# First branch's projection inside the last four attention rounds; value products one round back in three attentions

## Chip, cores and metric

The kernel runs on one core of one Trainium2 chip. The metric is the device time of one execution in microseconds. The kernel before was timed three times: median 3740.02 us, lowest 3732.03, highest 3750.38. The profile is of a fourth execution.

## What is computed

Batch 1, 256 tokens, width 1024. Four layers, fp32, in two blocks. The first block's two layers are feed-forward, mixer, feed-forward; the second block's two are mixer, mixture of experts. Only the mixers are touched by the change. Cut to what matters:

```python
# first block, layer 0 ("ab") and layer 1 ("cd"): 8 heads of 64
o = softmax(q k^T ...) @ v
x = x + m * (concatenate([att, conv]) @ w_out)

# second block, both layers
def mixer(h, ...):
    qa, ka, va, ub, qc, kc, vc, gates = split(h @ w_in)      # 28 slabs of 256 columns
    a = softmax(qk of map 0) - lam * softmax(qk of map 1)     # 4 heads, causal
    y_a = rms_norm(a @ va, subln_g) * (1 - lambda_init) @ w_proj_a
    y_b = silu(layer_norm(conv(glu(ub)))) @ w_proj_b + b_proj_b
    y_c = stick_breaking(qc, kc, vc) @ w_proj_c               # 8 heads
    g = sigmoid(gates)
    merged = g[0] * y_a + g[1] * y_b + g[2] * y_c
    return merged @ w_out
```

All layers also need modulation vectors: 9 (6 in the second block) vectors of 1024 per layer, each the product of a condition vector with a matrix from HBM.

## The kernel before

The program has ten sections s = 0 to 9, one after the other: ffn, ab, ffn, ffn, cd, ffn, mix2, moe, mix2, moe. Here "short mixers" are sections 1 (ab) and 4 (cd), written by `mixer1`; "long mixers" are sections 6 and 8, written by `mixer2`. Each engine has its own program, written by hand in the order in which the engine runs it, with semaphores between them (`wait_ge`, `then_inc`). What stands earlier in an engine's program always runs earlier. The activations lie transposed: 128 features on the partitions, 256 tokens along the row.

**Weights.** SyncE loads slabs of 1 MB into a ring of six slots, in program order; a slot is loaded again when the projection that read it six slabs before has signalled `proj_done`. In a long mixer slabs 0 to 27 are `w_in`, 28 and 29 the two halves of `w_proj_a`, 30 and 31 `w_proj_b`, 32 and 33 `w_proj_c`, 34 to 37 `w_out`. Results go to the PSUM banks 4 to 7 in turn: unit j to bank 4 + j % 4. Before unit j, TensorE waits for `proj_taken` (unit j - 4 has been read out of that bank). A long mixer's units 28 to 31 are the first branch (y_a), 32 to 35 the second, 36 to 39 the third; a unit is 8 matmuls.

**Short mixers' attention** (L1054 to L1090, ScalarE L1682 to L1691, VectorE L2269 on). For each of 8 heads: score of the next head, half a slab of `w_in` (rounds 0 to 5), four transposes of this head's probabilities (`turn_probs`, L1037) into bank 2, a copy of bank 2 to `pT` by ScalarE (`copy_turned`, L1660), and two value products from `pT` into bank 3 (`value`, L1075). In round 7 of section 1 the column sums of the next section's modulation (L891, 48 trace records) stand before the transposes.

**Long mixers' first attention** (L1153 to L1179). The same for four heads: scores of the next two maps, one whole slab (20 + i), transposes, value products (L1174), then slab 24, and the sums of squares of the output (`pairs`, L1029), which ScalarE squares first (L1641).

**Long mixers' second attention** (L1192 to L1212; VectorE `soft` L2466 on, L2485, L2490; ScalarE L1745 to L1771). Eight rounds i. TensorE: three suffix sums (L1200 to L1202), scores of head i + 2 (L1187, for i < 6), half a slab (L1205, for i < 4), and then a wait for `fin`, the product of VectorE (L2490) from which the value products (L1211) are made. VectorE, in rounds 0 to 3, ends with `scale_heads` (L2463, L2464), which finishes the first branch's input `ya` and signals `suba`; in rounds 4 to 7 with one modulation step (`add_mods`, L1992).

**Three projections** (L1214 to L1233). After the eight rounds TensorE runs the 12 units (L1231). VectorE (L2496 to L2519) first waits for `gsig`, ScalarE's sigmoid over the gates of branches 1 and 2 (L1774), and then takes unit after unit. In branch 0 each of its eight products (L2506) is followed by a modulation step, where there is one left: section 6 has eight left, section 8 none. In section 8 the column sums of the next modulation are split over two places of this stretch.

**Modulation steps.** GpSimd loads rows of `w_mod` (512 KB) into two buffers `wmod`, in turn (L821); a buffer is loaded again when VectorE has done the step that read it (`mod_step`).

Of the kernel before, what the change touches and what calls it, by code (L numbers as in the profile page):

```python
# [28 lines left out]
ACT = mybir.ActivationFunctionType  # L29
# [3 lines left out]
P = 128  # L33
# [207 lines left out]
def build(nc, A, out):  # L241
    ctx = ExitStack()
    with ctx:
# [582 lines left out]
        def _(pe):  # L826
# [213 lines left out]
            def mixer1(sec, X):  # L1040
# [40 lines left out]
                for i in range(NQ):  # L1081
# [8 lines left out]
                    value(i)  # L1090
# [31 lines left out]
            def mixer2(sec, X):  # L1122
# [36 lines left out]

                probs = lambda i: pb[:, (2 * i) % 4]  # L1160
# [3 lines left out]
                for i in range(4):  # L1164
# [5 lines left out]
                    pe.wait_ge(*X("pT_done", i + 1))  # L1170
                    if i:
                        pe.wait_ge(*X("o_taken", i))
                    for b in range(TB):
                        ins = pe.matmul(bank[3][:, 0:T], va(b, i), pT[:, i % 2, b, :], start=(b == 0), stop=(b == TB - 1))  # L1174
                    ins.then_inc(X["pv_done"], 1)
                slab(24)
# [3 lines left out]
                def z_scores(i):  # L1180
# [7 lines left out]
                    ins.then_inc(X["zs"], 1)  # L1188

# [4 lines left out]
                for i in range(8):  # L1194
# [10 lines left out]
                    if i < 4:  # L1205
                        slab(26 + i // 2, (i % 2,))
                    pe.wait_ge(*X("fin", i + 1))
# [6 lines left out]
                for br_, (ready, count, src) in enumerate((("suba", 4, ya), ("lnd", 1 + CT, glu), ("o_taken", 8, yc))):  # L1214
                    pe.wait_ge(*X(ready, count))
                    for half in range(2):
                        q = slabs[28 + 2 * br_ + half]
                        here(q)
                        w = proj_slab(q[0])
                        if (br_, half) == (1, 1) and s == 8:  # L1220
                            pe.wait_ge(*X("o_taken", 8))
                            pe.wait_ge(mod_step, MOD_STEPS * 9)
                            sum_columns(9, range(0, MODT // 2), 3)
                        if (br_, half) == (2, 0) and s == 8:
                            sum_columns(9, range(MODT // 2, MODT), 3, MODT // 2).then_inc(mod_summed, 1)
                        for m in range(4):
                            j = 28 + 4 * br_ + 2 * half + m // 2
                            if m % 2 == 0:
                                pe.wait_ge(proj_taken, taken0 + j - 3)
                            for k in range(CT):  # L1230
                                ins = pe.matmul(bank[4 + j % 4][:, (m % 2) * T:(m % 2 + 1) * T], w[:, k, m * P:(m + 1) * P], src[:, k, :], start=(k == 0), stop=(k == CT - 1))  # L1231
                            if m % 2:
                                ins.then_inc(proj_done, 1)  # L1233
# [1547 lines left out]
```

## Time and profile before

| | |
|---|---|
| median of 3 runs | 3740.02 us (3732.03 to 3750.38) |
| the profiled execution's own time | 3743.29 us |
| its span in the trace | 3741.5 us |
| mean granted TensorE clock | 0.969 of full speed |
| TensorE matmul busy | 3523.4 us (94%) |
| VectorE busy | 2328.0 us (62%) |
| ScalarE busy | 1464.8 us (39%) |
| moved by DMA | 842.64 MB, mean 225 GB/s |

The busy time of a pipelined engine counts a matmul from its issue to its modelled end, so rows of one group overlap: sixteen fp32 records of 128x256 take 3.62 us in a row of the timeline, but the next row starts 3.45 us after it. What a stretch costs is read from start to start. One fp32 matmul instruction of the program shows as two records, a transpose as one. In the timeline a bracket at a row's end gives the idle time before it and who ended it.

### The profile page before, as it was taken

To read this page: it belongs to the slowest core of one execution; us is meant where nothing else is said; L and a number is where in the kernel's file an instruction comes from. 1 tells how busy PE (TensorE), PEld (TensorE's weight loads), DVE (VectorE), ACT (ScalarE), POOL (GpSimd) and SP (SyncE) were. 2 spreads that over 40 slices of the span, in tenths; PEclk is the share of its full clock that TensorE was granted. 3 is DMA by queue.
4 is the path that set the end of the run, shared out by engine and by line. 5 is a ranking of instruction groups with operands and counts; after the bars stand their busy time and mean duration, and the time that the engine had idled before them with its cause. 6 is when DMAs were issued, how large, how long until landed. Compare 5 with 4: busy or idle time off the path is not lost.

```text
span 3741.5 us, 52688 instructions
## 1 busy us (share of the span) xinstructions
PE 3523.4 (94%) x21065; PEld 2988.2 (80%) x21065; DVE 2328.0 (62%) x3525; ACT 1464.8 (39%) x2213; POOL 246.2 (7%) x337
## 2 busy tenths in 40 slices
PE   4999999999899999899999999999888999999999
PEld 2998899997699877789777776778778977767776
DVE  6774476775477574456666666647454766666666
ACT  1432333432243214133555555531232345555554
POOL 3010010010001100000000000000000000000000
PEclk9999899999899999889999999999998999999999
DMA  7785385784278652345999989875322688999986
GB/s 265 254 293 184 98 285 191 253 299 151 76 259 297 208 169 93 133 157 181 295 302 299 297 266 297 282 241 169 132 84 92 214 272 277 295 282 299 296 278 197
DMA packets 580321, 842.64 MB, mean 225 GB/s; under 512 B 22715, under 2 KB 489760, under 8 KB 578832
## 3 DMA queue, kind: packets, MB, share of 16 engines
q1 hardware_dynamic: 514508, 665.85, 54.4%
q0 software_dynamic: 41056, 147.35, 11.7%
q10 hardware_dynamic: 24548, 26.57, 2.6%
q8 instruction: 141, 2.31, 0.3%
q14 instruction: 68, 0.56, 0.0%
HBM read 836.37 MB, written 3.33 MB: 224 GB/s over the span
## 4 chain that ended last, share of the span: by engine, by line
PE 75%; DVE 11%; DMA 8%; ACT 4%; issue 2%; SPq 1%; DVEq 0%; ACTq 0%
PE bank L1007 12%; PE bank L912 11%; PE bank L914 11%; PE bank L913 11%; PE bank L1366 8%; DMA ring<-in_w 3%; DMA far_up<-in_w 3%; DVE work L2400 2%; PE bank L1335 2%; PE bank L1379 2%; PE bank L1336 2%; PE bank L1231 2%; PE bank L1330 2%; PE bank L891 1%; PE bank L1331 1%
## 5 line engine op out<-in xcount | busy, mean ns | idle before, releaser
L914 PE MATMUL bank<-hh,ring_lo 128*128 128x256 f32 (+1 forms) x2176 | 621.2, 285 | 0.0
L912 PE MATMUL bank<-hh,hi 128*128 128x256 f32 (+1 forms) x1984 | 571.4, 288 | 13.2 <-issue 10.2
L913 PE MATMUL bank<-h_lo,hi 128*128 128x256 f32 (+1 forms) x1984 | 566.3, 285 | 0.0
L1007 PE MATMUL bank<-h,ring 128*128 128x256 f32 x2432 | 554.2, 388 | 7.4 <-DVE h L2513 3.9
L1007 PEld LDWEIGHTS bank<-h,ring 128*128 128x128 f32 x2432 | 474.0, 195 | 79.1 <-issue 7.0
L914 PEld LDWEIGHTS bank<-hh,ring_lo 128*128 128x128 f32 (+1 forms) x2176 | 419.3, 193 | 0.0
L912 PEld LDWEIGHTS bank<-hh,hi 128*128 128x128 f32 (+1 forms) x1984 | 382.2, 193 | 27.6 <-issue 21.3
L913 PEld LDWEIGHTS bank<-h_lo,hi 128*128 128x128 f32 (+1 forms) x1984 | 382.3, 193 | 1.4 <-issue 1.4
L912 PE MATMUL bank<-hid,hi 128*128 128x256 f32 (+1 forms) x1216 | 347.2, 286 | 1.1 <-DVE ring_lo L2660 1.1
L913 PE MATMUL bank<-hid_lo,hi 128*128 128x256 f32 (+1 forms) x1216 | 344.6, 283 | 0.0
L914 PE MATMUL bank<-hid,ring_lo 128*128 128x256 f32 (+1 forms) x1088 | 308.4, 283 | 0.0
L2655 DVE TENSOR_TENSOR ring_lo<-ring,hi_far 128x1024 fp32r<-128x1024 f32 x176 | 209.1, 1222 | 64.2 <-ACT hi_far L1817 63.6
L2126 DVE TENSOR_TENSOR ring_lo<-ring,hi 128x1024 fp32r<-128x1024 f32 (+1 forms) x180 | 209.3, 1199 | 55.0 <-ACT hi L1559 54.9
L912 PEld LDWEIGHTS bank<-hid,hi 128*128 128x128 f32 (+1 forms) x1216 | 233.9, 192 | 1.4 <-issue 1.2
L913 PEld LDWEIGHTS bank<-hid_lo,hi 128*128 128x128 f32 (+1 forms) x1216 | 233.9, 192 | 0.0
L2655 DVE TENSOR_TENSOR ring_lo<-ring,hi 128x1024 fp32r<-128x1024 f32 x168 | 199.8, 1222 | 41.9 <-ACT hi L1817 40.9
L1992 DVE SCALAR_TENSOR_TENSOR macc<-wmod,cond,macc 128x1024 f32<-128x1024 f32 x126 | 160.8, 1282 | 102.4 <-DMA wmod<-in_w_mod 88.5
L821 POOL DMA_DIRECT2D wmod<-in_w_mod x216 | 114.2, 529 | 1663.5 <-DVE macc L1992 963.3
L1559 ACT ACTIVATE hi<-ring 128x1024 fp32r<-128x1024 f32 (+1 forms) x180 | 180.5, 1035 | 110.2 <-DMA ring<-in_ffn_w 84.4
L795 POOL DMA_INDIRECT got<-rows_scratch,slot_tok x98 | 98.5, 1005 | 1700.4 <-PE bank L1317 1258.2
L914 PEld LDWEIGHTS bank<-hid,ring_lo 128*128 128x128 f32 (+1 forms) x1088 | 209.3, 192 | 0.0
L1817 ACT ACTIVATE hi_far<-ring 128x1024 fp32r<-128x1024 f32 x176 | 178.2, 1057 | 66.1 <-DMA ring<-in_w 66.1
(382 smaller groups left out, 6700.1 us busy)
## 6 DMA issues: line engine op xcount, KB each, us to landing
ring<-in_w SPq DMA_DIRECT2D x258, 1024.0 KB, 9.1
ring<-in_ffn_w SPq DMA_DIRECT2D x120, 1024.0 KB, 6.7
wmod<-in_w_mod POOLq DMA_DIRECT2D x216, 512.0 KB, 5.5
far_up<-in_w SPq DMA_DIRECT2D x84, 1024.0 KB, 11.3
ring<-in_w_in SPq DMA_DIRECT2D x74, 1024.0 KB, 5.2
work<-in_w SPq DMA_DIRECT2D x42, 1024.0 KB, 7.2
ring<-in_w_out SPq DMA_DIRECT2D x16, 1024.0 KB, 5.1
ring<-in_w_mod SPq DMA_DIRECT2D x12, 1024.0 KB, 12.1
```

What stands on the lines that cost most here:

```text
L795: pool.indirect_dma_start(got[0:m, p % 2, :], None, rows_dram[l].ap(), bass.IndirectOffsetOnAxis(slot_tok[0:m, rank - WIDE_FROM:rank - WID ...
L821: pool.dma_start(wmod[:, q % 2, :], w[l][k][:, at:at + D]).then_inc(mod_full[q % 2], 16)
L912: pe.matmul(o, w_hi, x_hi, start=start, stop=False, skip_group_check=True)
L913: pe.matmul(o, w_hi, x_lo, start=False, stop=False, skip_group_check=True)
L914: return pe.matmul(o, w_lo, x_hi, start=False, stop=stop, skip_group_check=True)
L1007: ins = pe.matmul(o[:, half * T:(half + 1) * T], l_, r_, start=(k == 0), stop=(k == KD - 1))
L1366: ins = pe.matmul(bank[2 + half][0:m, :], hidden_few[p % 2][:, c * m:(c + 1) * m], w[:, c, half * 512:(half + 1) * 512], start=(c == 0), s ...
L1559: act.activation(up_hi(j, t, m), up_half(slots[j], t, m), ACT.Copy).then_inc(hi_done, 1)
L1817: act.activation(up_hi(j, t, P, n % 2), unit_up(slot)[:, j, :, t * P:(t + 1) * P], ACT.Copy).then_inc(hi_done, 1)
L1992: dve.scalar_tensor_tensor(out=acc, in0=w, scalar=c, in1=acc, op0=ALU.mult, op1=ALU.add).then_inc(mod_step, 1)
L2126: dve.tensor_tensor(up_half(slots[j], t, m, ring_lo), up_half(slots[j], t, m), up_hi(j, t, m), ALU.subtract).then_inc(lo_done, 1)
L2655: dve.tensor_tensor(unit_up(slot, True)[:, j, :, c], unit_up(slot)[:, j, :, c], up_hi(j, t, P, n % 2), ALU.subtract).then_inc(lo_done, 1)
```

## The change

Three edits.

1. Short mixers: `value(i - 1)` comes behind `turn_probs(i)`, and `value(7)` behind the loop; ScalarE takes the results one round later (`take_values`).
2. Long mixers' first attention: the same, with `value(3)` between the two halves of slab 24.
3. Long mixers' second attention: in rounds 4 to 7 units 28, 29, 30 and 31 of the first branch's projection stand before the wait for `fin`, where rounds 0 to 3 have half a slab. The rest of the projections follows the loop as before. VectorE waits for `gsig` before branch 1 and no longer before branch 0.

```diff
@@ mixer1, TensorE
                     turn_probs(X, i, probs(i))
-                    value(i)
+                    if i:
+                        value(i - 1)
+                value(NQ - 1)
...
@@ mixer2, TensorE
+                def value(i):
+                    pe.wait_ge(*X("pT_done", i + 1))
+                    if i:
+                        pe.wait_ge(*X("o_taken", i))
+                    for b in range(TB):
+                        ins = pe.matmul(bank[3][:, 0:T], va(b, i), pT[:, i % 2, b, :], start=(b == 0), stop=(b == TB - 1))
+                    ins.then_inc(X["pv_done"], 1)
...
                     slab(20 + i)
                     turn_probs(X, i, probs(i))
-                    pe.wait_ge(*X("pT_done", i + 1))
                     if i:
-                        pe.wait_ge(*X("o_taken", i))
-                    for b in range(TB):
-                        ins = pe.matmul(bank[3][:, 0:T], va(b, i), pT[:, i % 2, b, :], start=(b == 0), stop=(b == TB - 1))
-                    ins.then_inc(X["pv_done"], 1)
-                slab(24)
+                        value(i - 1)
+                slab(24, (0,))
+                value(3)
+                slab(24, (1,))
...
+                def project(br_, half, src, pairs_of):
+
+                    q = slabs[28 + 2 * br_ + half]
+                    here(q)
+                    w = proj_slab(q[0])
+                    for pair in pairs_of:
+                        j = 28 + 4 * br_ + 2 * half + pair
+                        pe.wait_ge(proj_taken, taken0 + j - 3)
+                        for m in (2 * pair, 2 * pair + 1):
+                            for k in range(CT):
+                                ins = pe.matmul(bank[4 + j % 4][:, (m % 2) * T:(m % 2 + 1) * T], w[:, k, m * P:(m + 1) * P], src[:, k, :], start=(k == 0), stop=(k == CT - 1))
+                        ins.then_inc(proj_done, 1)
...
                     if i < 4:
                         slab(26 + i // 2, (i % 2,))
+                    else:
+
+                        pe.wait_ge(*X("suba", 4))
+                        project(0, (i - 4) // 2, ya, (i % 2,))
                     pe.wait_ge(*X("fin", i + 1))
...
-                for br_, (ready, count, src) in enumerate((("suba", 4, ya), ("lnd", 1 + CT, glu), ("o_taken", 8, yc))):
...
+                pe.wait_ge(*X("lnd", 1 + CT))
+                project(1, 0, glu, (0, 1))
+                if s == 8:
+                    pe.wait_ge(*X("o_taken", 8))
+                    pe.wait_ge(mod_step, MOD_STEPS * 9)
+                    sum_columns(9, range(0, MODT // 2), 3)
+                project(1, 1, glu, (0, 1))
+                pe.wait_ge(*X("o_taken", 8))
+                if s == 8:
+                    sum_columns(9, range(MODT // 2, MODT), 3, MODT // 2).then_inc(mod_summed, 1)
+                for half in range(2):
+                    project(2, half, yc, (0, 1))
                 pe.wait_ge(*X("merged", 1))
@@ mixer1, ScalarE
+                def take_values(n):
+
+                    act.wait_ge(*X("pv_done", 2 * n + 2))
+                    act.activation(att[:, n, :], bank[3][:, 0:T], ACT.Copy).then_inc(X["o_taken"], 1)
...
                     copy_turned(X, i, i - 1 if i >= 2 else 0)
+                    if i in (2, 4, 6):
+                        take_values(i // 2 - 1)
                     if i in (1, 3, 5):
                         take(sec, 6 + i // 2)
-                    if i % 2:
-                        act.wait_ge(*X("pv_done", i + 1))
-                        act.activation(att[:, i // 2, :], bank[3][:, 0:T], ACT.Copy).then_inc(X["o_taken"], 1)
+                take_values(NQ // 2 - 1)
@@ mixer2, ScalarE
                     copy_turned(X, i, i - 1 if i >= 2 else 0)
-                    act.wait_ge(*X("pv_done", i + 1))
-                    act.activation(ya[:, i, :], bank[3][:, 0:T], ACT.Copy).then_inc(X["o_taken"], 1)
+                    if i:
+                        take_values(i - 1)
+                take_values(3)
@@ mixer2, VectorE
-                dve.wait_ge(*X("gsig", 1))
                 for br_ in range(3):
+                    if br_ == 1:
+                        dve.wait_ge(*X("gsig", 1))
```

The order of instructions at the places of which the prediction speaks. In section 1, TensorE, the end of the last attention round and the start of the output projection (L891 are the column sums, L1037 the transposes, L1075 the value products, L1007 the output projection), a piece of the difference:

```order
 L891 MATMUL bank<-mats,macc 128x1 x24
 L1037 MATMUL bank<-mats,pb 128x128 x4
-L1075 MATMUL bank<-pT,vp 128x256 x2
+L1075 MATMUL bank<-pT,vp 128x256 x4
 L1007 MATMUL bank<-work,ring 128x256 x4
 L1007 MATMUL bank<-h,ring 128x256 x4
```

The value products of heads 6 and 7 now stand together behind the last transposes.

In section 6, TensorE, from the value products of round 5 of the second attention to the projections, before (L1200 to L1202 suffix sums, L1211 value products, L1231 projections, L1007 the output projection):

```order
L1211 MATMUL bank<-pT,vp 128x256 x2
L1200 MATMUL bank<-work,mats 128x256
L1201 MATMUL bank<-work,mats 128x256
L1202 MATMUL bank<-work,mats 128x256
L1211 MATMUL bank<-pT,vp 128x256 x2
L1200 MATMUL bank<-work,mats 128x256
L1201 MATMUL bank<-work,mats 128x256
L1202 MATMUL bank<-work,mats 128x256
L1211 MATMUL bank<-pT,vp 128x256 x2
L1231 MATMUL bank<-work,ring 128x256 x96
L1007 MATMUL bank<-h,ring 128x256 x48
```

The same place with the change (L1221 to L1223 are the suffix sums, L1236 the value products, L1208 the projections):

```order
L1236 MATMUL bank<-pT,vp 128x256 x2
L1221 MATMUL bank<-work,mats 128x256
L1222 MATMUL bank<-work,mats 128x256
L1223 MATMUL bank<-work,mats 128x256
L1208 MATMUL bank<-work,ring 128x256 x8
L1236 MATMUL bank<-pT,vp 128x256 x2
L1221 MATMUL bank<-work,mats 128x256
L1222 MATMUL bank<-work,mats 128x256
L1223 MATMUL bank<-work,mats 128x256
L1208 MATMUL bank<-work,ring 128x256 x8
L1236 MATMUL bank<-pT,vp 128x256 x2
L1208 MATMUL bank<-work,ring 128x256 x64
```

Eight of the projection's matmuls stand ahead of each value product of rounds 6 and 7, as in rounds 4 and 5 ahead of this piece, and 64 are left behind the rounds where there were 96.

## Rows read from the trace of the kernel before

**Rows 1.** Page: the chain that ended last, share of the span by engine.

```profile
PE 75%; DVE 11%; DMA 8%; ACT 4%; issue 2%; SPq 1%; DVEq 0%; ACTq 0%
```

**Rows 2.** Source view of L1075: idle before it (both TensorE rows), us, times.

```profile
  ACT pT L1660: 26.1, 32
```

**Rows 3.** TensorE timeline, section 1, round 0: start, duration, operation, records, [idle].

```profile
345.46 3.62 PE L1007 MATMUL bank<-h,ring 128*128 128x256 f32 x16
348.91 0.60 PE L1037 MATMUL bank<-mats,pb 128*128 128x128 f32 x4
350.20 1.13 PE L1075 MATMUL bank<-pT,vp 128*128 128x256 f32 x4 [0.69 <-ACT pT L1660]
351.17 0.59 PE L1065 MATMUL bank<-kz,work 128*128 128x256 f32 x2
```

**Rows 4.** TensorE timeline, section 1, rounds 6 and 7, output projection.

```profile
392.19 0.66 PE L1037 MATMUL bank<-mats,pb 128*128 128x128 f32 x4 [1.96 <-DVE pb L2287]
...
395.40 10.24 PE L891 MATMUL bank<-mats,macc 128*128 128x1 f32 x48
405.50 1.09 PE L1037 MATMUL bank<-mats,pb 128*128 128x128 f32 x4
...
409.83 3.78 PE L1007 MATMUL bank<-work,ring 128*128 128x256 f32 x8 [0.47 <-ACT work L1691]
```

**Rows 5.** VectorE timeline, section 4, its wait in a round.

```profile
927.55 0.69 DVE L2273 TENSOR_REDUCE small<-bank 128x2 f32<-128x512 f32 x1 [1.11 <-PE bank L1065]
```

**Rows 6.** TensorE timeline, section 4, the last round's transposes.

```profile
953.64 1.11 PE L1037 MATMUL bank<-mats,pb 128*128 128x128 f32 x4 [2.43 <-DVE pb L2287]
```

**Rows 7.** TensorE timeline, section 6, first attention, round 0.

```profile
1409.74 0.60 PE L1037 MATMUL bank<-mats,pb 128*128 128x128 f32 x4
...
1412.05 1.89 PE L1157 MATMUL bank<-kz,work 128*128 128x256 f32 x8
```

**Rows 8.** ScalarE timeline, section 6: the square behind the last copy.

```profile
1443.34 0.38 ACT L1736 ACTIVATE work<-bank 128x256 f32<-128x256 f32 x1 [1.22 <-PE bank L1174]
1443.76 1.06 ACT L1641 ACTIVATE work<-work 128x1024 f32<-128x1024 f32 x1
```

**Rows 9.** TensorE timeline, section 6, rounds 4 to 7 and projections.

```profile
1488.24 0.59 PE L1200 MATMUL bank<-work,mats 128*128 128x256 f32 x2
...
1493.01 1.13 PE L1211 MATMUL bank<-pT,vp 128*128 128x256 f32 x4 [2.44 <-DVE pT L2490]
...
1506.16 2.07 PE L1211 MATMUL bank<-pT,vp 128*128 128x256 f32 x4 [3.31 <-DVE pT L2490]
...
1513.78 25.48 PE L1231 MATMUL bank<-work,ring 128*128 128x256 f32 x112
...
1547.44 17.10 PE L1231 MATMUL bank<-work,ring 128*128 128x256 f32 x64 [3.37 <-DVE work L2504]
```

**Rows 10.** VectorE timeline, section 6, round 7 and first branch.

```profile
1512.12 1.28 DVE L1992 SCALAR_TENSOR_TENSOR macc<-wmod,cond,macc 128x1024 f32<-128x1024 f32 x1
1519.37 0.42 DVE L2506 TENSOR_TENSOR h<-bank,work 128x256 f32<-128x256 f32 x1 [5.96 <-ACT work L1774]
...
1544.64 1.28 DVE L1992 SCALAR_TENSOR_TENSOR macc<-wmod,cond,macc 128x1024 f32<-128x1024 f32 x1 [4.34 <-issue]
```

**Rows 11.** Windows view, 1506 to 1509: busy per engine (instructions), granted clock, DMA share, GB/s.

```profile
1506.00:1509.00 3.00, 2.84 (x7) 2.28 (x8) 1.30 (x2) 0.00 (x0) 0.53 (x1) 0.50 0.07 12
```

**Rows 12.** Tile view of wmod, 1440 to 1560: time of its loads.

```profile
DMA to landing us min/median/max: 3.5/4.0/6.7
```

**Rows 13.** DMA view, 1513 to 1546: KB each, median us to landing.

```profile
ring<-in_w_out SPq DMA_DIRECT2D x4, 1024.0 KB, 7.1
```

**Rows 14.** TensorE timeline, section 8, round 4, projections, column sums.

```profile
2747.07 0.59 PE L1200 MATMUL bank<-work,mats 128*128 128x256 f32 x2
...
2772.15 22.57 PE L1231 MATMUL bank<-work,ring 128*128 128x256 f32 x96
...
2806.74 14.06 PE L1231 MATMUL bank<-work,ring 128*128 128x256 f32 x64
```

More of the change, by code:

```diff
@@ L1212, in mixer2 @@
                     ins.then_inc(X["pv_done"], 1)
-                for br_, (ready, count, src) in enumerate((("suba", 4, ya), ("lnd", 1 + CT, glu), ("o_taken", 8, yc))):
[L1215 to L1233, printed above, removed]
+                pe.wait_ge(*X("lnd", 1 + CT))
[10 more added lines that the diff above has]
+                    project(2, half, yc, (0, 1))
                 pe.wait_ge(*X("merged", 1))
@@ L1725, in exps, with take_values @@
                     exp_scores(X, pb[:, i % 4], pb[:, i % 4], i % 4, i % 2)
+                def take_values(i):
+                    act.wait_ge(*X("pv_done", i + 1))
+                    act.activation(ya[:, i, :], bank[3][:, 0:T], ACT.Copy).then_inc(X["o_taken"], 1)
                 exps(0)
```

## The prediction

> **What bounds the kernel now.** I read the page's chain first: three quarters of it is TensorE [rows 1], so time is won where TensorE has nothing to do or runs slowly in the mixers. The source view of the short mixers' value products gives 26.1 us of idle time, both TensorE rows counted, in 32 cases: each of the 16 rounds waits for ScalarE's copy of the transposes [rows 2]. The timelines show the size of each place. In a round of section 1 the transposes start at 348.91, the value products at 350.20, the next score at 351.17 [rows 3]. Sixteen records of the slab before them take 3.45 us from start to start where their row says 3.62 [rows 3]; so a record is 0.216 us, a program's matmul 0.43, and the last 0.17 us of a row lie under the next. In rounds 4 to 7 of the second attention there is no slab to run, and TensorE waits 2 to 3 us for VectorE's product (2.44 and 3.31 in the rows) [rows 9]. The windows view shows what else this costs: in one such stretch the granted clock is 0.50, 1.2 of 2.4 GHz [rows 11].
>
> **Short mixers, rounds 0 to 5.** From transposes to next score takes 2.26 us; without the wait it is 0.43 (0.60 less 0.17) and 0.86 (four records), 1.29. That is 0.97 a round, 5.8 us in six rounds. The cover of the copy is the next head's work. In section 1 nothing else is near. In section 4 VectorE idles only 1.11 us a round [rows 5]: the 0.97 just fits.
>
> **Section 1, rounds 6 and 7.** From the transposes of round 6 at 392.19 to the output projection at 409.83: 17.6 us [rows 4], with the 48 records of column sums at half speed (10.24, so 5.1 at full). After: transposes 0.43, value(5) 0.86, column sums between 5.1 and 10.2, I take 7.7, since a 0.7 us gap is gone ahead of them; transposes at half speed 0.86, value(6) and value(7) 1.73 each, 0.7 to ScalarE's copy and back: 14.0. Gain 3.6; all at half 1.1, all at full 8.2. Section 1: **9.4** (6.9 to 14.0).
>
> **Section 4, rounds 6 and 7.** Here VectorE decides: TensorE waits 2.43 us for it before the last transposes [rows 6], and value(5) goes into that wait for nothing. Behind it value(6) now stands ahead of value(7): at half speed 1.73 us where the wait was 0.7 plus a refill, a loss of 0.6; at full speed a gain of 1.0. I take -0.3. Section 4: **5.5** (4.5, if VectorE's slack falls short by 0.15 in each round, to 6.8).
>
> **First attention of the long mixers.** 1409.74 to 1412.05 is 2.31 us [rows 7] against 1.29: 1.02 in each of four rounds, **4.1** per section. value(3) stands between the halves of slab 24, and the squares wait for it: copy and square end at 1444.82, 1.5 us after the copy's start [rows 8], and 3.45 us of the second half cover them.
>
> **Second attention and projections.** A piece of projection is eight matmuls, 3.45 us. A round with it and with scores is 3 x 0.43 + 0.86 + 3.45 + 0.86 = 6.48 us, without scores 5.6. In round 4 value products could start 4.77 us after the round's start (1488.24, 1493.01) [rows 9]; with the piece they start at 5.6 and without scores at 4.75, so VectorE's product is ready or nearly. Rounds 4 to 7 become 2 x 6.48 + 2 x 5.6 = 24.2 us; now they take 25.5 in section 6 (to 1513.78) and 25.1 in section 8 (2747.07 to 2772.15) [rows 9, 14]. The filler is longer than the waits in rounds 4 and 5; what pays is that 32 matmuls, 13.8 us, are gone behind the loop.
>
> Section 8: now 2747.07 to 2820.8 (2806.74 + 14.06) [rows 14], 73.7 us. After: 24.2, then 0.5 for the bank of unit 28, which VectorE frees after round 7's modulation step (1.28) and two products (0.42 each) while the value products run, then 64 matmuls at 27.6 and the column sums at 5.2, 57.6 with the seams. Gain 16.1; down to 12 if the clock costs as much as behind a wait of section 6 (3.3, below). The sigmoid of ScalarE now comes due before branch 1: VectorE idled 5.96 us for it [rows 10], but the first branch's takes and four banks lie between. Section 8: **20.1** (16.1 to 20.1).
>
> Section 6: VectorE also has eight modulation steps here, one behind each product of the first branch. They were late already: the first product at 1519.37, the last step at 1544.64, TensorE held until 1547.44 [rows 9, 10]. After, they start with round 7's own step, now 1512.12 [rows 10], 1.4 us earlier like the round, so its end is 1512.0; VectorE no longer waits for the sigmoid. But only one of the two buffers is full then. The other's chain is four loads and four steps: 4 x (0.3 + L + 1.28), L from issue to landing. The view says 3.5 / 4.0 / 6.7 for L [rows 12]. With 4.5 the last step ends at 1536.3; with 4.0 at 1534.3; at the pace of before (7 steps in 24.8 us, and 4 us for the missing buffer) at 1542.3. I take 1536.3, because four loads of 1 MB with 7.1 us each ran beside the steps [rows 13], and of these two now leave SyncE's queue in rounds 5 and 7. GpSimd's loads start some 6 us earlier and nothing is queued behind them. TensorE stands still in between, for units 33 to 35, and resumes freely at 1538.3 (two products and two sums of branch 1). The last 32 matmuls take 13.8 at full speed; they took 17.10 [rows 9]; I take 15.5. End 1553.8, now 1564.5: 10.7, with 0.3 of shorter seams **11.0**. Ends: 14.7 (1534.3 and full speed) and 3.1 (1542.3 and 17.1).
>
> The Trainium skill (DMA: Bandwidth & Descriptors, Issuing engines are not separate DMA queues) says that transfers of all issuing engines run on the same 16 engines and interleave. By it the two slab loads that move ahead slow the modulation loads of rounds 5 to 7 instead, and section 6 would keep only the lower end, 3.1. The spread of L between 3.5 and 6.7 agrees that sharing costs [rows 12]; that it costs as much in the rounds, where DMA share is 0.07 in a window [rows 11], does not follow.
>
> **Sum.** 9.4 + 5.5 + (4.1 + 11.0) + 20.1 = 50.1 us, bounds 35 and 60. The profiled execution took 3743.3 (span 3741.5), 3.3 above the median. 3743.3 - 50.1 = 3693.2, and on the median 3740.0 - 50.1 = 3689.9: **3690 us**. What comes behind the mixers waits for them and shifts along.
>
> **Rivals.** (a) *The modulation loads decide section 6.* They keep last place wherever VectorE starts, and nothing of the 11.0 comes: 3740 - 39 = 3701. For it: the 4.34 us wait ahead of the last step [rows 10]. Against: they also waited for the sigmoid. Chance 0.13.
>
> (b) *The fillers do not fill.* The value products wait as long as before, after the piece, because a product or a bank comes late: 8 pieces x 3.45 = 27.6 lost, 3740 - 22.5 = 3717.5; the change would then not do what it says. Against: 4.77 us from the round's start to the product. Chance 0.04.
>
> (c) *Given back later.* The next sections' first weights or loads are late by what the mixers gained, and half of it goes: 3715 to 3723. The chain's DMA share of 8% speaks for it [rows 1]; against, that each load waits for TensorE's release and moves along. Chance 0.05.
>
> (d) *The clock, slower than before.* Section 6 now has about three waits of 2.5 to 3 us, one before each of units 33 to 35. In the rounds before, waits of this size ended in a granted clock of 0.50 [rows 9, 11]. If it stayed there from round 4 to the end of the output projection (24.2 + 27.6 + 27.6 us at full speed), that stretch costs 79 us more: 3740 - 50 + 79 = 3769. It decides from 69 us of such work at half speed. Against: the work between the waits is as long as the waits. Chance 0.02. The Trainium skill (TensorE: Matmul & The Clock Gate, HAM oscillation) tells of kernels whose groups all ran at half rate because of repeated waits; by it section 6 alone would give rival (d).
>
> The forecast case has 0.74, and 0.02 are left for gains beyond 60.
>
> **Numbers.** The forecast's bounds give 3680 to 3705; single runs of this kernel lie up to 10 us from the median (3732 to 3750), and rival (a) lies inside: 3672 to 3712. A measurement can tell about 0.5%, 18.7 us, from no change. Faster by more than that (below 3721.3): forecast, (a), the tail and most of (b) and (c), 0.92. Within 0.5%: the rest of those, 0.05. Slower: (d) and what I don't see, 0.03.
>
> **What would show it.** Value products of the short mixers and the first attention without idle time before them, except in round 7; rounds of 5.6 us (section 4) and 6.5 (section 1). In rounds 4 to 7 of the long mixers a row of 16 projection records each, no waits of 2 us, granted clock 1.00, and 64 matmuls behind round 7. In section 8 from round 4 to the projections' end 57 to 59 us. In section 6 TensorE idle before units 33 to 35, the last modulation step some 9 us earlier against round 4 than now. Wrong would be: VectorE's products later than the pieces' ends; granted clock of 0.50 through the projections; section 4's rounds still at 6.57; mixture-of-experts sections longer by what the mixers gained.

## The result and the profile after

| | before | changed |
|---|---|---|
| median, us | 3737.48 (4 runs, 3732.03 to 3750.38) | 3691.83 (4 runs, 3689.15 to 3699.27) |
| ratio, 95% interval | | 0.987 (0.985 to 0.989) |
| the profiled execution's own time | 3743.29 | 3699.27 |
| its span | 3741.5 | 3697.5 |

A second measurement of both (`after_again` below) gave 3688.78 and 3741.38 us, ratio 0.9855 (0.9832 to 0.9879). The forecast was 3690 (3672 to 3712). Two executions ran far slower than all others, at a lower granted clock, and every ratio leaves them out: one of the kernel before (4537.73 us) and the profiled one of `proj_only` (9984.95 us).

The 44 us between the two profiled executions are 1.2% of the span, too little to be read from the page's chain [rows 1], which has TensorE at 75% in both. The gain is read at the places themselves. Source view of the short mixers' value products (L1075), changed kernel:

```profile
its engine sat idle before it (us, times) until:
who waited for it (us, times):
```

Nothing stands under the first line, where 26.1 us in 32 cases stood [rows 2]. TensorE timeline of the changed kernel, section 1, round 0, and then rounds 6 and 7 to the output projection:

```profile
349.84 0.60 PE L1037 MATMUL bank<-mats,pb 128*128 128x128 f32 x4
350.28 0.60 PE L1065 MATMUL bank<-kz,work 128*128 128x256 f32 x2
...
386.55 0.66 PE L1037 MATMUL bank<-mats,pb 128*128 128x128 f32 x4 [1.96 <-DVE pb L2314]
387.04 1.36 PE L1075 MATMUL bank<-pT,vp 128*128 128x256 f32 x4
388.20 10.24 PE L891 MATMUL bank<-mats,macc 128*128 128x1 f32 x48
398.30 1.09 PE L1037 MATMUL bank<-mats,pb 128*128 128x128 f32 x4
399.18 2.92 PE L1075 MATMUL bank<-pT,vp 128*128 128x256 f32 x8
402.57 1.99 PE L1007 MATMUL bank<-work,ring 128*128 128x256 f32 x8 [0.47 <-ACT work L1702]
```

The next score follows the transposes after 0.44 us, without a gap [rows 3]. The column sums still run at half speed, 10.24 us [rows 4]; the output projection no longer does, 1.99 us for eight records where 3.78 stood.

Section 4 of the changed kernel: the same instruction of VectorE as in [rows 5], in two rounds and in the last one, then TensorE's last transposes and the output projection:

```profile
915.91 0.69 DVE L2300 TENSOR_REDUCE small<-bank 128x2 f32<-128x512 f32 x1
...
921.40 0.69 DVE L2300 TENSOR_REDUCE small<-bank 128x2 f32<-128x512 f32 x1
...
931.70 0.69 DVE L2300 TENSOR_REDUCE small<-bank 128x2 f32<-128x512 f32 x1 [0.22 <-PE bank L1065]
```

```profile
938.07 1.11 PE L1037 MATMUL bank<-mats,pb 128*128 128x128 f32 x4 [3.38 <-DVE pb L2314]
938.98 3.62 PE L1075 MATMUL bank<-pT,vp 128*128 128x256 f32 x8
...
971.50 1.97 PE L1007 MATMUL bank<-work,ring 128*128 128x256 f32 x8 [1.93 <-issue]
```

VectorE's wait of 1.11 us in a round [rows 5] is gone: the first two rows are 5.49 us apart and have no idle time before them, while TensorE's rounds take 5.62. So the slack was just enough, and the rounds took the whole gain. TensorE's wait for VectorE in the last round grew from 2.43 [rows 6] to 3.38.

Section 6, TensorE of the changed kernel: first attention, a round of the second attention without scores, round 7 and the projections:

```profile
1391.41 0.60 PE L1037 MATMUL bank<-mats,pb 128*128 128x128 f32 x4
1391.85 1.89 PE L1159 MATMUL bank<-kz,work 128*128 128x256 f32 x8
...
1478.85 0.59 PE L1221 MATMUL bank<-work,mats 128*128 128x256 f32 x2
...
1480.14 3.62 PE L1208 MATMUL bank<-work,ring 128*128 128x256 f32 x16
...
1484.58 0.59 PE L1221 MATMUL bank<-work,mats 128*128 128x256 f32 x2
...
1489.33 1.03 PE L1236 MATMUL bank<-pT,vp 128*128 128x256 f32 x4
1491.49 3.69 PE L1208 MATMUL bank<-work,ring 128*128 128x256 f32 x16 [1.13 <-DVE h L2534]
1499.09 5.41 PE L1208 MATMUL bank<-work,ring 128*128 128x256 f32 x16 [3.91 <-DVE h L2534]
1505.38 3.69 PE L1208 MATMUL bank<-work,ring 128*128 128x256 f32 x16 [0.89 <-DVE h L2534]
1513.20 19.22 PE L1208 MATMUL bank<-work,ring 128*128 128x256 f32 x80 [4.13 <-DVE h L2534]
1534.38 3.90 PE L1007 MATMUL bank<-h,ring 128*128 128x256 f32 x9 [1.97 <-DVE h L2541]
```

Round 6 lasts 5.73 us and has no wait of 2 us; round 7's value products end at 1490.4. But the wait has not gone, it stands behind the loop: TensorE idles for the banks of units 32 to 35, 1.13, 3.91, 0.89 and 4.13 us. The two waits of about 4 us are each followed by a slow stretch: 16 records take 5.41 us instead of 3.62, and 80 records 19.22 where 17.5 is the pace of the others, some 1.8 us each. Behind the two short waits the records run at full speed. Who holds the banks is in VectorE's timeline of the same kernel (the last two of the eight steps):

```profile
1511.52 1.28 DVE L2019 SCALAR_TENSOR_TENSOR macc<-wmod,cond,macc 128x1024 f32<-128x1024 f32 x1 [3.50 <-issue]
...
1513.40 1.28 DVE L2019 SCALAR_TENSOR_TENSOR macc<-wmod,cond,macc 128x1024 f32<-128x1024 f32 x1 [0.26 <-DVE h L2534]
```

The projection's products stand behind the modulation steps. "Issue" says that the profile ties the steps' wait to no event, but the loads can be set beside them. GpSimd's timeline of the changed kernel has the issue of the last load; the tile view of `wmod` for 1507.5 to 1508.4 has the time to its landing, and the same view for 1420 to 1520 that of ten loads:

```profile
1507.98 0.53 POOL L821 DMA_DIRECT2D wmod<-in_w_mod  x1 [2.26 <-DVE macc L2019]
```

```profile
DMA to landing us min/median/max: 5.3/5.3/5.3
```

```profile
DMA to landing us min/median/max: 3.8/4.9/6.2
```

The last load lands at 1513.3, and the last step starts at 1513.40: the steps start when their loads land. The median of the loads was 4.0 us before [rows 12]. Of the ten here, the five issued while a slab's load was under way took 5.3 to 6.3 us, the other five 3.8 to 4.5. The steps come 3.4 us apart on average (1489.72 to 1513.40, seven intervals). Section 8 has no steps left here. TensorE, from the value products of round 7 (round 4 began at 2710.30):

```profile
2733.73 1.03 PE L1236 MATMUL bank<-pT,vp 128*128 128x256 f32 x4
2734.69 7.14 PE L1208 MATMUL bank<-work,ring 128*128 128x256 f32 x32
2741.67 2.73 PE L891 MATMUL bank<-mats,macc 128*128 128x1 f32 x24
2744.27 7.15 PE L1208 MATMUL bank<-work,ring 128*128 128x256 f32 x32
2751.26 2.73 PE L891 MATMUL bank<-mats,macc 128*128 128x1 f32 x24
2753.85 14.06 PE L1208 MATMUL bank<-work,ring 128*128 128x256 f32 x64
2769.88 2.74 PE L1007 MATMUL bank<-h,ring 128*128 128x256 f32 x6 [1.97 <-DVE h L2541]
```

It ends at 2767.9, 57.6 us behind round 4, where it was 73.7 [rows 14]. Windows view of the changed kernel, rounds 4 to 7 of section 6 and its waits; columns as in [rows 11]:

```profile
1466.00:1490.00 24.00, 24.00 (x113) 20.91 (x111) 16.64 (x24) 6.97 (x12) 1.94 (x4) 1.00 0.46 154
1490.00:1513.00 23.00, 13.15 (x50) 10.05 (x48) 10.92 (x14) 6.57 (x4) 3.34 (x7) 0.93 0.74 251
```

In the rounds the granted clock is 1.00 (2.4 GHz) where [rows 11] had 0.50, and the DMA share is 0.74 where TensorE now waits.

### The profile page after: what moved, and what is told of

Same layout as the page of the kernel before. It is cut to its first block, busy times and chain, and to the rows that moved or that the text cites. A ratio compares the mean times of both kernels' runs of the same rounds, so it can differ in the third digit from the quotient of the medians.

```text
span 3697.5 us, 52694 instructions
## 1 busy us (share of the span) xinstructions
PE 3505.3 (95%) x21065; PEld 2980.5 (81%) x21065; DVE 2327.4 (63%) x3525; ACT 1464.5 (40%) x2213; POOL 248.9 (7%) x337
## 3 DMA queue, kind: packets, MB, share of 16 engines
q1 hardware_dynamic: 514508, 665.85, 55.3%
## 4 chain that ended last, share of the span: by engine, by line
PE 75%; DVE 10%; DMA 9%; ACT 3%; issue 2%; SPq 1%; DVEq 0%; ACTq 0%
PE bank L1007 12%; PE bank L912 11%; PE bank L913 11%; PE bank L914 11%; PE bank L1383 8%; DMA ring<-in_w 4%; DMA far_up<-in_w 3%; DVE work L2427 2%; PE bank L1352 2%; PE bank L1396 2%; PE bank L1353 2%; PE bank L1208 2%; PE bank L1347 2%; PE bank L891 1%; PE bank L1348 1%
## 5 line engine op out<-in xcount | busy, mean ns | idle before, releaser
L912 PE MATMUL bank<-hh,hi 128*128 128x256 f32 (+1 forms) x1984 | 571.7, 288 | 13.8 <-issue 10.2
L1007 PE MATMUL bank<-h,ring 128*128 128x256 f32 x2432 | 553.3, 387 | 7.4 <-DVE h L2541 3.9
L1007 PEld LDWEIGHTS bank<-h,ring 128*128 128x128 f32 x2432 | 472.7, 195 | 78.4 <-issue 6.7
```

Source lines behind the costliest of these rows:

```text
L912: pe.matmul(o, w_hi, x_hi, start=start, stop=False, skip_group_check=True)
L1007: ins = pe.matmul(o[:, half * T:(half + 1) * T], l_, r_, start=(k == 0), stop=(k == KD - 1))
```

## The experiments

All twelve runs in four groups. "Tail" is from the start of round 4 to the output projection's start, "section" from a section's first matmul to the next one's.

### Each edit alone

`short_only` is the kernel before with edit 1 (TensorE's part):

```diff
-                    value(i)
+                    if i:
+                        value(i - 1)
+                value(NQ - 1)
```

> Edit 1 alone (value products one round back in sections 1 and 4). Theory A (each part's gain is local and stays): the sections shorten as in the trace of the changed kernel, 9.9 us in section 1 and 8.0 in section 4, and the whole by 18, with the sections of experts as long as before. Theory B (the sections of experts give part back whenever they start earlier): sections 1 and 4 as in A, but section 7 and 9 together longer by 6 to 12 us, the whole better by only 6 to 12. My forecast had 14.9 for this part.

`first_only` is the kernel before with edit 2 (TensorE's part):

```diff
+                    if i:
+                        value(i - 1)
-                slab(24)
+                slab(24, (0,))
+                value(3)
+                slab(24, (1,))
```

> Edit 2 alone (value products one round back in the first attention of sections 6 and 8). Theory A: 4.1 us in each section, 8 in all, no other section changed. Theory B: the same in the sections, and less or nothing of it left at the end.

`proj_only` and, for a second profile, `proj_again` are the kernel before with edit 3, VectorE's moved wait included (its first piece):

```diff
+                    else:
+                        pe.wait_ge(*X("suba", 4))
+                        project(0, (i - 4) // 2, ya, (i % 2,))
```

> Edit 3 alone (first branch's projection in rounds 4 to 7). Theory A: from round 4 to the end of the projections 9.8 us less in section 6 and 16.1 in section 8, 26 in the whole, and granted clock 1.00 in rounds 4 to 7. Theory B: the same in the sections, but only 14 to 20 in the whole. Rival on section 8, which got 24.3 us shorter where the first attention and the projections explain 20.2: if the other 4 come from this edit, they show here too; if they are chance or belong to edit 2, they don't.

> Edit 3 alone once more, for its profile; the profiled execution of the last one ran at a granted clock of 0.338 throughout and tells nothing. Round 4 to output projection: 68.5 us in section 6 and 59.6 in section 8 (78.3 and 75.7 before), rounds 4 to 7 at 6.48, 6.48, 5.73, 5.6 and granted clock 1.00. Sections 1 and 4 as before (142 to 148 and 166.6 us).

| | median, us | ratio to before (3741.41) | less, us | forecast terms |
|---|---|---|---|---|
| short_only | 3722.26 | 0.9951 (0.9932 to 0.9970) | 18 (11 to 25) | 14.9 |
| first_only | 3735.61 | 0.9988 (0.9972 to 1.0004) | 4 (-1 to 10) | 8.1 |
| proj_only | 3722.42 | 0.9945 (0.9927 to 0.9963) | 21 (14 to 27) | 27.1 |

"Less" is 3741.41 times (1 - ratio). The sum is 43 us, the changed kernel lost 49 and 54 in its two measurements: the three edits add up within their intervals, and none of the three alone carries the result. Theory A's 18 us for edit 1 came. For edit 3 the interval holds both theory A's 26 and theory B's 14 to 20. `first_only` can't be told from no change by its time; its trace shows the term: from the first score of the first attention to the sums of squares 51.66 us in section 6 and 51.65 in section 8, where the kernel before has 54.3 to 57.2.

`proj_again`, one run, 3733.02 us, has rounds 4 to 7 as expected (24.4 us) and tails of 67.8 and 64.6 us in sections 6 and 8. Section 8's is 5 us above the 59.6 that were expected: behind the column sums 32 records take 8.84 us instead of 7.15, and 64 take 17.12 instead of 14.06. The second is also in the kernel before (17.05 in `before_again`) and so not the edit's. The first is in four of the seven traces that have edit 3 and in none of the six others; whether the edit has a part in it is open. The 4 us that the rival looked for in section 8 did not show.

The expectation of `proj_again` says that the profiled execution of `proj_only` ran at 0.338 throughout. That is its mean. Windows view of `proj_only`:

```profile
79.00:1760.00 1681.00, 1607.61 (x10691) 1502.08 (x10690) 1063.78 (x1665) 551.71 (x841) 103.57 (x193) 0.96 0.61 202
1766.50:6394.00 4627.50, 4621.27 (x4375) 3095.95 (x4375) 570.04 (x797) 409.11 (x590) 56.15 (x69) 0.16 0.16 51
```

Up to 1760 us, inside section 7, the clock is 0.96 as elsewhere, and sections 1 to 6 can be read: 141.6 us in section 1, 166.7 in section 4, and a tail of 66.5 us in section 6. Why the clock then fell to 0.16 is open. The mean with `proj_again` is 67.2 us for edit 3 alone in section 6, against 77.6 in the kernel before and 67.5 in the changed one, so edit 3 carries the whole of this term.

### Section 6: are the modulation steps the wait?

`mods_moved` is the changed kernel, with two steps behind each `combine` of section 6's first attention, so that none are left for the projections:

```diff
                     combine(i)
+                    if s == 6:
+                        add_mods(2, MADE_IN[s][1])
```

> The changed kernel, with the eight modulation steps behind the first branch's products of section 6 done two per round in its first attention instead. Theory C (these steps and their loads hold TensorE before units 32 to 35): the waits there go, the stretch from round 4 to the end of the projections takes 52 to 53 us instead of 66.5, and the whole gains 14 over the changed kernel, about 3678. Rival D (TensorE waits for banks because VectorE's products themselves, or the sigmoid, are late): the stretch stays at 62 or more. Rival E (VectorE has no room in the first attention, or the loads collide with slabs there): the tail shortens by 14 and the first attention grows by 5 to 14.

`mods_moved_again`, `after_again`: the same kernel and the changed one side by side.

> The changed kernel with section 6's modulation steps begun in the first attention, for a direct comparison with the changed kernel on one chip. If the steps are what holds section 6 back: section 6 is 14 to 18 us shorter than in the changed kernel's trace and the median 12 to 18 us below that of the changed kernel. If the first measurement owed its 10 us to the chip: within 3 us of it.

> The changed kernel once more, for a second trace and as the partner of the next two. Theory 1 (the expert sections vary by themselves, nothing is given back): ratio to the kernel before 0.985 to 0.989; in the trace sections 7 and 9 anywhere from 890 to 900 and 896 to 907 us, section 1 at 132 or 138 us by the granted clock of its column sums. Theory 2 (the experts give back part of the mixers' gain): sections 7 and 9 again longer by 3.6 and 8.9 us than in the traces of the kernel before, within 1 us each.

Measured: `mods_moved` 3681.53 us, ratio to before 0.9851 (0.9818 to 0.9884). Side by side on one chip 3676.66 us, 0.9827 (0.9798 to 0.9856), against 3688.78 for the changed kernel: 12 us less by the medians of six runs each, whose intervals overlap, so that the traces say it more firmly than the times. TensorE timeline of `mods_moved`, section 6, round 7 and the projections:

```profile
1479.62 3.62 PE L1208 MATMUL bank<-work,ring 128*128 128x256 f32 x16
1483.07 1.03 PE L1236 MATMUL bank<-pT,vp 128*128 128x256 f32 x4
1484.03 27.86 PE L1208 MATMUL bank<-work,ring 128*128 128x256 f32 x128
1513.85 11.45 PE L1007 MATMUL bank<-h,ring 128*128 128x256 f32 x44 [1.96 <-DVE h L2543]
```

All 64 matmuls run in one piece, 27.86 us, as fast as the forecast priced them; the tail is 54.2 us in both traces, against 68.5 and 66.6. Rival D falls with it, and rival E too: the first attention takes 50.2 us from the first score to the sums of squares, and 51.7 and 50.3 in the changed kernel. Section 6 as a whole is 342.9 us beside 353.5 and, in the changed kernel's first trace, 357.5, so 11 and 15 us less; 14 to 18 were expected. The steps, and through them the loads, hold section 6. Does that need the change? `before_mods` does the same to the kernel before:

> The kernel before with the eight modulation steps of section 6 done two per round in its first attention. Theory C (the steps hold TensorE): in the kernel before they cost only what TensorE waited for banks, 1.1 and 3.4 us, and a slow start behind it, so 3 to 5 us, and the whole 3733 to 3737. If it gains 14 as in the changed kernel, the move of the steps is worth the same without the change and my account of the tail is wrong.

3739.12 us, 1.0002 (0.9988 to 1.0015), and not the 3733 to 3737 of theory C. In its one trace the tail of section 6 is 70.4 us, against 75.6 to 78.8 in three traces of the kernel before, so 5 to 8 us less, but the whole gained nothing that can be measured; where the tail's gain goes is open. With the filled rounds the same move takes 13 us from the tail.

### What the pieces and the moved wait are worth

`fill_last_two` is the changed kernel with only units 28 and 29 inside, in rounds 6 and 7; 30 and 31 stand behind the loop:

```diff
-                    else:
+                    elif i > 5:
                         pe.wait_ge(*X("suba", 4))
-                        project(0, (i - 4) // 2, ya, (i % 2,))
+                        project(0, 0, ya, (i % 2,))
...
+                project(0, 1, ya, (0, 1))
                 pe.wait_ge(*X("lnd", 1 + CT))
```

> The changed kernel with the projection's pieces only in rounds 6 and 7 (units 28 and 29); units 30 and 31 behind the loop. Theory G (what pays is work taken out from behind the loop, less what a piece is longer than its wait): rounds 4 and 5 fall back to waits of 2.44 us and 5.73, which is 0.75 each less than 6.48, and 6.9 us stand behind the loop again: section 8 loses 5.4 us against the changed kernel, 65.0 from round 4 to the output projection. Rival H (what pays is mainly the granted clock, which the waits pull down): two waits of 2.44 us cost 2 to 4 us more, 67 to 69. In section 6 it is less, 0 to 5, since the modulation steps decide there.

3703.48 us, 0.989 (0.9866 to 0.9913). Section 8's tail is 69.8 us, 10.2 more than in the first trace of the changed kernel (59.6) and 8.6 more than in the second (61.3): above theory G's 65.0 and above rival H's 67 to 69. Section 6's is 68.3, within 1 of the changed kernel's mean (67.5). TensorE timeline of `fill_last_two`, section 8, end of round 4 and of round 5, and behind the loop:

```profile
2724.88 2.08 PE L1236 MATMUL bank<-pT,vp 128*128 128x256 f32 x4 [2.44 <-DVE pT L2518]
...
2732.24 1.13 PE L1236 MATMUL bank<-pT,vp 128*128 128x256 f32 x4 [2.44 <-DVE pT L2518]
...
2744.55 13.98 PE L1208 MATMUL bank<-work,ring 128*128 128x256 f32 x64
...
2760.96 8.84 PE L1208 MATMUL bank<-work,ring 128*128 128x256 f32 x32
...
2772.24 15.75 PE L1208 MATMUL bank<-work,ring 128*128 128x256 f32 x64
```

The waits of 2.44 us are back and the rounds 4 to 7 are no shorter for it (24.4 us in both kernels). Theory G had 1.5 us less for them; what a piece is longer than its wait is eaten by the slow records behind the first wait (2.08 us for four, 1.13 behind the second), which is rival H's point, at 1.6 us. So in rounds 4 and 5 a piece is free. Behind the loop stand 32 records more, 6.9 us, as in theory G. Against the changed kernel's first trace the rest, 3.4 us, is in two places behind the column sums: 8.84 instead of 7.15 us, and 15.75 instead of 14.06. TensorE timeline of `after_again`, the same place:

```profile
2738.98 8.84 PE L1208 MATMUL bank<-work,ring 128*128 128x256 f32 x32
```

The first of the two is there as well, and the second, 15.75 us, in `gsig_early`, both with all pieces inside. So neither needs pieces to be missing. In section 6 the same pieces buy nothing, since the steps end last.

`gsig_early` is the changed kernel with VectorE's wait for the sigmoid ahead of branch 0 again:

```diff
+                dve.wait_ge(*X("gsig", 1))
                 for br_ in range(3):
-                    if br_ == 1:
-                        dve.wait_ge(*X("gsig", 1))
```

> The changed kernel, with VectorE's wait for the sigmoid ahead of branch 0 again. My theory: VectorE then takes units 28 to 31 only after ScalarE's sigmoid, which ended some 6 us behind the last attention round; TensorE has units 28 to 31 done in the rounds and needs the bank of unit 28 for unit 32 right behind the loop, so it stands still: 3 to 5 us more in section 8 and, since the steps start later too, 3 to 5 us more in section 6; 6 to 10 us above the changed kernel. Rival (the sigmoid is done in time, since ScalarE has the rounds for it, and the moved wait buys nothing): within 2 us of the changed kernel.

3708.91 us, 0.9915 (0.9891 to 0.9939), 20 us more than the changed kernel beside it and more than the 6 to 10 that were expected. TensorE timeline of `gsig_early`, section 8, behind round 7, and VectorE's wait there:

```profile
2733.88 1.03 PE L1236 MATMUL bank<-pT,vp 128*128 128x256 f32 x4
2741.31 9.33 PE L1208 MATMUL bank<-work,ring 128*128 128x256 f32 x32 [6.41 <-DVE h L2533]
```

```profile
2740.28 3.63 DVE L2533 TENSOR_TENSOR h<-bank,work 128x256 f32<-128x256 f32 x8 [6.39 <-ACT work L1801]
```

The kernel before has nearly the same wait of VectorE, 5.96 us [rows 10], and TensorE does not feel it, since four banks take the 32 matmuls that follow the loop. With these inside the loop all four banks are full when it ends, and VectorE's 6.39 us become TensorE's 6.41, with a slower clock behind it (9.33 us where 7.14 stood). The tails are 72.5 and 69.9 us, so 5.9 and 8.7 more than `after_again`'s 66.6 and 61.3: 14.6 us, more than half of what edit 3 gains. The other 5 us of the 20 are not at this place: in the one pair of traces section 8 reaches round 4 5.8 us later, a stretch that lies between 257 and 268 us in all of them; whether the edit has a part in it is open.

### Given back later?

`before_again` and `before_third` are the kernel before, for its sections.

> The kernel before, unchanged, profiled once more. Theory F (the lengths of the expert sections differ from run to run by chance): section 7 between 890 and 895 us, section 9 between 896 and 907, and not the values of the first trace again (890.7 and 896.2) to within a tenth. Theory B (expert sections give back what the mixers gain): both as in the first trace, 890.7 and 896.2, within 1 us.

> The kernel before once more, for a third trace of it, with the expert sections. If they vary by themselves, one of them should be over 893 or 899 us; if they are always short under the mixers before, both are again within 1.5 us of 891 and 896 us.

One run each, 3739.26 and 3742.21 us. Lengths of sections in every trace, us (of `proj_only` up to the fall of its clock):

| | 1 | 4 | 6 | 7 | 8 | 9 |
|---|---|---|---|---|---|---|
| before | 148.0 | 166.6 | 373.3 | 890.7 | 365.6 | 896.2 |
| before_again | 141.6 | 166.8 | 369.7 | 891.9 | 364.5 | 896.4 |
| before_third | 141.6 | 166.8 | 373.0 | 898.6 | 360.4 | 896.8 |
| changed | 138.0 | 158.6 | 357.5 | 894.2 | 341.3 | 905.1 |
| after_again | 138.0 | 158.6 | 353.5 | 894.8 | 341.1 | 901.8 |
| mods_moved | 132.1 | 158.3 | 339.6 | 894.9 | 341.2 | 898.9 |
| mods_moved_again | 132.2 | 158.3 | 342.9 | 894.5 | 344.8 | 905.6 |
| gsig_early | 132.1 | 158.4 | 360.4 | 887.8 | 353.9 | 899.4 |
| fill_last_two | 139.3 | 158.1 | 356.9 | 894.9 | 353.5 | 906.7 |
| short_only | 138.0 | 158.6 | 370.1 | 894.6 | 368.8 | 898.5 |
| first_only | 141.6 | 166.7 | 366.3 | 890.8 | 358.0 | 906.6 |
| proj_again | 146.2 | 166.4 | 360.3 | 899.7 | 352.3 | 903.2 |
| proj_only | 141.6 | 166.7 | 362.6 | | | |
| before_mods | 141.6 | 166.7 | 363.0 | 897.4 | 365.8 | 902.9 |

Section 7 varies by itself: 890.7 to 898.6 in three executions of one kernel, and shortest, 887.8, in a kernel with the mixers changed. Section 9 is another matter: 896.2 to 896.8 in the three traces of the kernel before, 898.5 to 906.7 in the ten others. It is not in proportion to what the mixers gained: `before_mods`, whose whole is unchanged, has 902.9, `mods_moved`, the shortest trace, 898.9. Windows view of section 9, before and changed; columns as in [rows 11]:

```profile
2845.30:3741.50 896.20, 855.91 (x5053) 672.35 (x5051) 568.57 (x829) 437.52 (x641) 48.82 (x49) 0.99 0.81 256
```

```profile
2792.40:3697.50 905.10, 860.79 (x5053) 674.68 (x5051) 568.76 (x829) 436.99 (x641) 50.45 (x49) 0.98 0.80 254
```

The same work runs with the granted clock at 0.98 instead of 0.99 and 4.9 us more of TensorE's busy time, and the rest is waiting. So some 2 to 10 us do go in section 9, also where the mixers gained nothing in the whole, and why is open.

## Why the prediction was right, by its steps

**Sum.** 50.1 us forecast. The ratios give 49 and 54 us, within the bounds. That it came so close is in part luck. In the first pair of traces the four mixers gave 58 us (10.0, 8.0, 15.8 and 24.3 in sections 1, 4, 6 and 8), 8 more than forecast, and sections 7 and 9 took 3.5 and 8.9 more, which no term had: the profiled execution came out 44 us shorter. Over all traces of the two kernels it is some 57 us won and some 8 lost. Two errors of about one size and opposite sign meet in the total.

**Section 1, 9.4.** Measured 10.0 between the two traces with slow column sums (148.0, 138.0) and 9.5 between those with fast ones (141.6, 132.1). The parts were not as told. The rounds gave 6.6 us, not 5.8: rounds 0 to 5 hold the value products of five heads now and not of six, and the forecast charged the sixth (value(5)) behind them without taking it out of them. From the transposes of round 6 to the output projection it was 1.6 us and not 3.6, since the column sums stayed at 10.24 us and were not 7.7. The output projection's first rows at full speed, 1.8 us, were in no term. (The bound for all at full speed adds up to a gain of 8.4, not 8.2.)

**Section 4, 5.5.** Measured 8.0 to 8.2, above the upper bound of 6.8. The term that was mis-sized is the rounds, 6.6 us and not 5.8, by the same slip: value(5) does go "into that wait for nothing", so the 0.86 us that it leaves in rounds 0 to 5 come back nowhere. The output projection's first rows at 1.97 us instead of 3.62, also in no term, gave the rest. The value products of two heads at half speed cost what was said, 3.41 us from start to start for twice 1.73.

**First attention, 4.1 per section.** 1.02 us in each round is what the timeline shows. From the first score to the sums of squares the three traces of before have a mean of 55.3 (section 6) and 56.3 (section 8), the two of the changed kernel 51.0 and 51.1: 4.3 and 5.2.

**Rounds and projections, section 8, 16.1.** Rounds 5.7 and 6.5 us, 24.4 in all, 57.6 to the end: exactly the sum, in the first trace. In the second it is 59.3, by 32 slow records behind the column sums (8.84 us for 7.15), which the forecast did not have. Over all traces the tail goes from 76.3 to 60.4, 15.8. But "the first branch's takes and four banks lie between" hid a condition: it holds only with the moved wait. Weighed alone by `gsig_early` it is worth 8.7 us there, and the text priced it nowhere.

**Section 6, 11.0.** 9.8 against the first trace, 10.0 over all. The last step ended 48.8 us behind round 4's start (1514.7 less 1465.9), the forecast said 48.1 (1536.3 less 1488.2). Three waits of TensorE were forecast, before units 33 to 35; there were four, the first of them (1.13 us) before unit 32. The Trainium skill's rule on shared DMA engines (DMA: Bandwidth & Descriptors, Issuing engines are not separate DMA queues), that transfers interleave on the same engines whoever issues them, agrees with the trace: beside a slab's load a `wmod` load takes 5.3 to 6.3 us, otherwise 3.8 to 4.5. The 3.1 us that the forecast derived from it did not come, 10 us came.

**Rivals.** (a) The loads decide section 6: half true. They do end last, `mods_moved` shows 12 us for them; but they began earlier too, which the rival denied. (b) fell: all pieces fill. (c) fell in its form; section 9's 2 to 10 us stand in its place, unexplained. (d) fell: the clock is 0.93 over the waits and 1.00 in the rounds. It did drop behind the two waits of about 4 us, for 1.8 us of lost time each, and came back both times. The Trainium skill (TensorE: Matmul & The Clock Gate, HAM oscillation) tells of a kernel that dropped in every group, with some 2 us of matmuls between waits of 3 to 5; here pieces of 3.7 to 5.4 us stood between waits of 0.9 to 4.1, so that the forecast's "by it section 6 alone would give rival (d)" read the section too broadly.

**The best version.** `mods_moved`, 3676.66 us: 1.7% below the kernel before, and by the medians about 12 us below the change.

## What to carry to other kernels

A wait in a loop is filled with work of the next stage, and then the next stage's first wait must be looked at anew: here all four banks are full when the loop ends, and a wait on another engine that four empty banks had hidden becomes TensorE's own, 6.4 us of it. Price such a companion edit by itself, since the main edit's sum holds only with it. Where an accumulation fed by loads stands between an engine and the banks that it has to free, start it a stage earlier: in the whole no gain that can be measured before the change, about 12 us after it.

## What was not expected of the hardware

The same code shows two lengths of section 1, with the column sums' 48 records at 10.24 us or near 6. TensorE timeline of `mods_moved`, whose column sums were fast:

```profile
389.19 1.03 PE L1075 MATMUL bank<-pT,vp 128*128 128x256 f32 x4
390.06 5.75 PE L891 MATMUL bank<-mats,macc 128*128 128x1 f32 x48
```

Which of the two comes is not set by the kernel: the kernel before has 148.0 and twice 141.6 us, and with edit 1 four traces have 138.0 to 139.3 and three 132.1 or 132.2. A term of 6 us is thus drawn anew in each execution, and a difference between two single traces has to be read with that in mind. Section 8 has a smaller one of the kind: the projection's records behind its column sums lose between nothing (the first traces of both kernels) and 5 us (`proj_again`).
